# A fused transformer block and two hybrid layers on one core: norm roots on token columns, the key root one unit later, and another order in the second layer's lead

## The reference

```python
def rmsnorm(x, g):
    return x * lax.rsqrt(jnp.mean(x * x, axis=-1, keepdims=True) + 1e-6) * g
def first_block(...):
    h = rmsnorm(x, attn_pre_g)                       # stage "pre"
    ...                                              # attention of 16 heads
    x = x + rmsnorm(mix, attn_post_g)                # stage "post"
    h = rmsnorm(x, mlp_pre_g)                        # stage "mpre"
    y = (gelu(conv(h @ w_gate)) * (h @ w_up)) @ w_down
    x = x + rmsnorm(y, mlp_post_g)                   # stage "mpost"
    return x + (p @ w_ple) * sigmoid(x @ w_ple_gate)
def hybrid_layer(...):                               # two of them, on 16 meta tokens + 512
    h = rms_norm(x, norm_g)
    q, k, v, gate_a, u_b, gate_b, q_idx, k_idx, w_idx, merge = split(h @ w_in)
    q, k = rope(rms_norm(q)), rope(rms_norm(k)); q_idx, k_idx = rope(q_idx), rope(k_idx)
    score = sum_h relu(q_idx_h @ k_idx.T) * w_idx_h * scale
    sel = top_k(where(visible, score, -1e30), 128)
    attn = softmax over sel of (q @ k.T) @ v
    y_a = (attn * silu(gate_a)) @ w_a
    y_b = (multiscale_pool(u_b) * silu(gate_b)) @ w_b
    return x + (sigmoid(m_a) * y_a + sigmoid(m_b) * y_b) @ w_out
```

## Time and profile before

| | |
|---|---|
| median of 3 runs | 1642.54 us (1640.53 to 1642.84) |
| profiled execution, its own time | 1645.56 us |
| its span | 1643.6 us |
| granted TensorE clock, mean | 0.97 |
| PE busy | 1533.8 us (93%) |
| POOL busy | 1084.2 us (66%) |
| DVE busy | 945.4 us (58%) |
| ACT busy | 507.2 us (31%) |

### The profile page before, as it was taken

One profiled execution on the slowest core, in us unless ns is written; L12 is line 12 of the kernel. 1 busy time (PEld: TensorE's weight loads), 2 busy tenths in 40 slices (PEclk: granted clock), 3 DMA queues, 4 the chain that ended last, 5 costly groups with the idle time before them and its releaser, 6 DMA issues.

```text
span 1643.6 us, 26709 instructions
## 1 busy us (share of the span) xinstructions
PE 1533.8 (93%) x9622; PEld 1278.3 (78%) x9622; DVE 945.4 (58%) x2013; ACT 507.2 (31%) x1244; POOL 1084.2 (66%) x1700
## 2 busy tenths in 40 slices
PE   6989878979999999997999999999999988999999
PEld 4766544747777777885799988888999977788999
DVE  5544655067676763007686778863547769874251
ACT  3243565232111111003356333332125623333210
POOL 6542400749999998787987656445888853455685
PEclk9998988989999999998999999999999998999999
DMA  6120000212222223222222212111222211121223
GB/s 233 52 65 26 27 1 1 67 49 89 84 83 88 89 89 103 92 96 70 83 78 78 75 63 70 52 52 59 90 91 78 78 65 41 51 75 55 72 93 105
DMA packets 37351, 119.56 MB, mean 73 GB/s; under 512 B 5376, under 2 KB 7552, under 8 KB 36992
## 3 DMA queue, kind: packets, MB, share of 16 engines
q1 hardware_dynamic: 35824, 115.74, 21.2%
q10 hardware_dynamic: 1424, 2.41, 0.4%
HBM read 116.02 MB, written 2.10 MB: 72 GB/s over the span
## 4 chain that ended last, share of the span: by engine, by line
PE 70%; DVE 12%; POOL 8%; issue 4%; ACT 4%; DMA 0%; POOLq 0%; ACTq 0%; SPq 0%; DVEq 0%
PE ps L665 54%; POOL wlo L578 6%; PE ps L684 3%; POOL whi L574 2%; PE ps L1068 2%; DVE score L2100 2%; PE ps L824 2%; DVE score L2099 2%; PE ps L758 2%; PE ps L678 1%; PE ps L1143 1%; PE ps L691 1%; ACT pts L1337 1%; PE ps L1138 1%; ACT probs L1324 1%
## 5 line engine op out<-in xcount | busy, mean ns | idle before, releaser
L578 POOL TENSOR_TENSOR wlo<-raw,whi 128x256 fp32r<-128x256 f32 x752 | 606.4, 838 | 15.7
L574 POOL TENSOR_SCALAR whi<-raw 128x256 fp32r<-128x256 f32 x752 | 365.3, 512 | 364.4 <-PE ps L665 352.1
L665 PE MATMUL ps<-hh,whi 128*128 128x512 f32 (+2 forms) x1736 | 574.1, 331 | 25.8 <-DVE hl L1893 9.3
L665 PE MATMUL ps<-hl,whi 128*128 128x512 f32 (+2 forms) x1736 | 559.2, 322 | 0.0
L665 PE MATMUL ps<-hh,wlo 128*128 128x512 f32 (+2 forms) x1736 | 558.6, 322 | 0.0
L665 PEld LDWEIGHTS ps<-hh,whi 128*128 128x128 f32 x1736 | 329.3, 190 | 83.1 <-POOL wlo L578 27.4
L665 PEld LDWEIGHTS ps<-hh,wlo 128*128 128x128 f32 x1736 | 329.5, 190 | 25.8
L665 PEld LDWEIGHTS ps<-hl,whi 128*128 128x128 f32 x1736 | 329.4, 190 | 24.9 <-issue 2.2
L665 PE MATMUL ps<-plain_high,whi 128*128 128x264 f32 (+2 forms) x288 | 84.1, 292 | 6.3 <-POOL wlo L578 5.9
L1715 DVE TENSOR_TENSOR tmp<-tmp 128x512 f32<-128x512 f32 x14 | 9.7, 696 | 136.3 <-ACT tmp L1407 101.9
L684 PE MATMUL ps<-const,probs 128*128 128x128 f32 x360 | 67.7, 315 | 20.6 <-DVE probs L1874 20.0
(11 more groups left out here) (311 smaller groups left out, 2722.7 us busy)
## 6 DMA issues: line engine op xcount, KB each, us to landing
raw<-in_w SPq DMA_DIRECT2D x200, 512.0 KB, 3.3
x<-in_x SPq DMA_DIRECT2D x4, 512.0 KB, 6.9
out<-x SPq DMA_DIRECT2D x8, 256.0 KB, 6.3
raw<-in_w SPq DMA_DIRECT2D x12, 128.0 KB, 2.8
raw<-in_w SPq DMA_DIRECT2D x4, 384.0 KB, 3.1
cw_k<-in_cw1k SPq DMA_DIRECT2D x1, 1024.0 KB, 5.5
cw_v<-in_cw1v SPq DMA_DIRECT2D x1, 1024.0 KB, 8.3
raw<-in_w SPq DMA_DIRECT2D x4, 256.0 KB, 3.2
```

What stands on the lines that cost most here:

```text
L574: ins = pool.tensor_scalar(whi[s][:, c:c + PIECE], raw[s][:, c:c + PIECE], 1.0, 0.0, ALU.mult, ALU.add)
L578: ins = pool.tensor_tensor(wlo[s][:, c:c + PIECE], raw[s][:, c:c + PIECE], whi[s][:, c:c + PIECE].bitcast(F32), ALU.subtract)
L665: mm = pe.matmul(out, lhs, rhs, start=start and n == 0, stop=stop and n == 2)
```

## The change

1. The stages pre, post and mpost take their root on token columns. PE sums each token's squares with 128x1 matmuls (`token_sums`), ACT takes the root of 128x4, DVE the reciprocal of 128x4 into `small`, and PE spreads it back over the partitions into the PSUM tile X (`spread_root`, four matmuls of 128x128 with the identity). `norm` multiplies by X. In mpost the third unit of `embedded` stands between the sum and the spreading. Stage mpre stays as it was.
2. In both layers the ones matmul and ACT's 128x528 root go. The reciprocal is of 128x5, PE spreads it within the value unit (`spread_halves`, six matmuls of up to 128x128), and ACT copies it to `keep`. The squares of the key are summed in 5 columns before the first query unit, the key's root is taken on 128x5, and PE spreads it after the second query unit. `kiT` is written without it, and `kT` in two multiplications by X before chunk 2's rotation (`keys_out`).
3. In layer 1 the lead has an order of its own for PE, ACT and DVE; the selection of tile 2 leaves the lead and is dealt to slots 0 and 1; tile 3's side steps move from slots 0 to 4 to slots 2 to 5, and tile 4's from 5 to 9 to 6 to 9.

```diff
-                lead = rest + named("ga0 ga1") + two[0:1] + named("ga2") + score_first + two[1:2] + [("weighted", 0)]
-                lead += named("ga3") + two[2:3] + named("mg0") + two[3:] + named("mg1")
+                lead = ga[0:2] + two[0:1] + ga[2:3] + score_first + ga[3:] + two[1:2] + mg[0:1] + two[2:3] + mg[1:] + two[3:]
+                lead_act = ga[0:2] + two[0:1] + ga[2:] + score_first + two[1:2] + mg[0:1] + two[2:3] + mg[1:] + two[3:]
+                lead_dve = rest + ga[0:2] + score_first + two[0:1] + ga[2:3] + [("weighted", 0)] + ga[3:] + two[1:]
+                side[0] += picks[0:4]
+                side[1] += picks[4:]
-                spans = [(3, 0, 5), (4, 5, 10)]
+                spans = [(3, 2, 6), (4, 6, 10)]
...
+            def token_sums(tag, src, outs, start=True, stop=True):
+                for t, out in enumerate(outs):
+                    mm = pe.matmul(out, src[:, t * P:(t + 1) * P], ones[:, 0:1], start=start, stop=stop)
+                return mm
+            def spread_root(tag):
+                pe.wait_ge(*at("token_rstd", tag))
+                for t in range(QT):
+                    mm = pe.matmul(X[:, 0, t * P:(t + 1) * P], small[:, 13, t:t + 1].to_broadcast([P, P]), ident,
+                                   start=True, stop=True)
+                mm.then_inc(*tick("rstd_spread", tag))
...
-            def norm(tag, src, normed, cols, gain, r, out=None, then=None):
+            def norm(tag, src, normed, cols, gain, out=None, then=None):
+                r = X[:, 0, :]
                 dve.wait_ge(*at("rms", tag))
-                dve.reciprocal(r, r).then_inc(*tick("rstd", tag))
-                dve.wait_ge(*at("rstd", tag))
+                dve.reciprocal(small[:, 13, 0:QT], small[:, 12, 0:QT]).then_inc(*tick("token_rstd", tag))
+                dve.wait_ge(*at("rstd_spread", tag))
...
             embedded(1)
-            sum_added("mpost", [X[:, 0, :]], [tmp[:, 2, 0:S]])
-            for m in range(2, DC):
+            sum_added("mpost", tmp[:, 2, 0:S])
+            embedded(2)
+            spread_root("mpost")
+            for m in range(3, DC):
...
+                        if (m, k) == (L_V, 2):
+                            pe.wait_ge(*at("token_rstd", tag))
+                            spread_halves(r_tok).then_inc(*tick("rstd_spread", tag))
...
                     if c == 1:
+                        pe.wait_ge(*at("k_token", l))
+                        spread_halves(k_tok[2]).then_inc(*tick("k_spread", l))
...
+                def keys_out():
+                    dve.wait_ge(*at("k_spread", l))
+                    for half in (1, 0):
+                        ins = dve.tensor_tensor(halves(kT2[half * HD:(half + 1) * HD, :]), halves(kT2[0:HD, :]),
+                                                X[0:HD, :, 0:TH], ALU.mult)
+                    ins.then_inc(*tick("k_ready", (l, 1)))
```

125 lines of the change are left out of this document (76 added, 49 removed).

## The result

The change is slower: 1650.75 us median of 5 runs (1648.78 to 1651.20) against 1640.94 of 5 (1640.53 to 1642.84); ratio 1.0045, interval 1.0031 to 1.0060, so 5 to 10 us (the two medians lie 9.8 apart). The forecast was 1625. The profiled execution has a span of 1649.0 us against 1643.6, granted clock 0.97 in both. The change's profile lies at its median, that of the kernel before 3 to 5 us above its own, so the two profiles differ by 5.4 only.

What follows compares the result with a forecast made beforehand. PE, busy 93% of the span, was taken as the bound; terms -2.2 (pre), -3.3 (post), -1.6 (mpost), -2.0 (heads) and -8.5 (lead) gave -17.6, from 1642.54 to 1625 us median, range 1617 to 1634.

Steps and rivals of the forecast that it cites:

- Pre, -2.2: Stage pre: shorter root and reciprocal in PE's chain against an added spreading, -2.4, less 0.2 for the clock: -2.2 us.
- the columns cost what the ones matmul did: Stages pre, post, mpost: ten one-column passes cost PE 1.17 us against 1.16 for four wide ones.
- Post, -3.3: Stage post: shorter chain -2.4, two shorter norms -1.05, with +0.2 for the clock: -3.3 us.
- the +0.2 for the clock: Stage post: slower clock of PE behind idling, priced at +0.2 us.
- Mpost, -1.6: Stage mpost: DVE starts 2.4 us earlier, a wait of some 0.5 within `embedded`, only later waits shrink: -1.6 us.
- Heads, -2.0: Heads of both layers: PE work +3.6 us, waits shrink by 5.6: -2.0 us.
- three quarters of the 7.3 for gone: Heads of both layers: of 7.3 us that PE stands behind POOL and in a further wait, 5.6 go.
- Lead to slot 3, -8.5: Layer 1 lead: first stall -5.5, its clock -2.6, second stall -6.7, new slot 2 stall +4.8, relu waits +1.5: -8.5 us.
- Slots 4 to 10, 0: Layer 1 from slot 3 on: PE has no wait of note, as DVE's remaining slots carry less than PE's; no cost.
- The rival on the slower side: Layer 1: dealt selection delays tile 3's, PE stands at slot 6; needs DVE over 22 us behind; say 1646; chance 0.03.
- roots are hidden or dear: Stages and heads: spreadings cost more, heads +3.6, stages at half; about -8, 1634 us; chance 0.12.
- The signs that the forecast named for a wrong step: PE waiting over 1 us at `embedded` or the key's spreading; the new wait at slot 2 over 9 us or absent.

Runs made afterwards that it cites:

- the run without dealing: The change with tile 2's selection back in the lead in one piece and the old spans for tiles 3 and 4: 1642.09 us, ratio 0.9996 to the kernel before.
- the third part alone: The kernel before with only the change's layer 1 lead orders, dealing of tile 2's selection and spans: 1648.81 us, ratio 1.0031.
- the half rounds: The change with 8 of the 16 rounds of tile 3's selection in layer 1 left out: 1643.23 us, ratio 0.9998 to the kernel before.
- the slot more for tile 3: Kernel before with four of tile 2's rounds in the lead, rest in slot 0; tile 3 in slots 1 to 5 instead of 1 to 4: 1635.53 against 1640.53 us.
- the relus first: The change with ACT taking index (4)'s relus in slot 6 ahead of the eviction and exponentials: 1650.39 us, ratio 1.0041 to the kernel before.
- half a move: Kernel before with another lead: four of tile 2's rounds in the lead, four in slot 0, tile 3 in slots 1 to 5: 1635.53 us, ratio 0.9961.
- Pre only: The kernel before with only stage pre on token columns as in the change: 1644.69 us, ratio 1.0009.
- the runs with roots, pre or heads only: Change without its third part, 1645.59 us; kernel before with only the change's stage pre, 1644.69 us; kernel before with only its two layer heads, 1644.93 us.

## Why the prediction was wrong

- **Pre, -2.2, measured +2.7 to +3.0 in the seven profiles that have it, +1.4 (-1.0 to +3.8) in the median.** The failed step is "the columns cost what the ones matmul did", with 0.2 for an engine that had just idled. At equal pace it holds (1.7 us a chunk for either, 0.95 and 1.02 in mpost). But the row that it was taken from ran at full clock, and so did the last chunks of pre before, behind wide passes. With columns the pace never rose: eight passes at 0.213 us stand against two at 0.43. That is 0.85 us in each of five chunks, 4.2 in all, and the spreading took 2.07 where the sum had 1.03.
- **Post, -3.3, measured -1.5.** The mechanism was right: the reciprocal and the relief of the norms came (the first norm to PE's first product took 4.18 instead of 5.11 us). The term mis-sized is the +0.2 for the clock: the columns took 1.87 where the ones sum had 1.13, and the spreading 2.08 where the sum had 1.03, together 1.8. Where a later kernel met full clock here, post gave -2.3 to -4.3, so the size of this term is in part chance.
- **Mpost, -1.6, measured -2.5.** The wait within `embedded` was 0.17, not 0.5, and the norms took 0.73 to 0.75. The relief of DVE's norms, by row and rule, came as forecast.
- **Heads, -2.0, measured +0.9 in the sections, +2.6 (0.3 to 4.9) in the median.** The failed step is "three quarters of the 7.3 for gone". POOL's waits went as forecast (5.9 to 1.5 in both layers), but the wait for DVE's fourth rotated query stands at 1.7 in each layer, where only layer 1 had one, of 1.4. So 2.4 us of waiting went, not 5.6. PE's busy time grew by 0.9 and 2.3, 3.2 against the 3.6 that the sum had, although a spreading took 1.5 to the next start where 1.25 was taken. (Three quarters of 7.3 is 5.5, a slip of 0.1.)
- **Lead to slot 3, -8.5, measured -8.2.** First stall and its clock gone, the new stall in slot 2 at 5.4 against 4.8; by kinds, 6.5 of idle time and 1.7 of slower work, where the sum had 5.9 and 2.6.
- **Slots 4 to 10, 0, measured +13.7.** This decides. The failed step: "From slot 3 on PE has no wait of note, today nor then, since DVE's remaining slots carry less than PE's". The trace of the kernel before speaks against it: DVE was busy for 23.83 of the 24.90 us of slots 3 to 5. Tile 3 and tile 4 have four slots each instead of five, and index (4) moved into a slot where ACT and DVE are not free for it. Three waits of 2 us came of it, and half clock was priced at nothing: it cost more than the waits, 8.7 of busy time against 2.9 + 2.0 of idle time. About half of that slower work also came in the run without dealing, which has none of the new waits.
- The rival on the slower side named the right mechanism, later selections behind the dealt one, but expected a stall for tile 3's mask at slot 6 and put it beyond a backlog of 22 us. No such stall came: waits for `gate_out`, a relu and an eviction did it, with half clock. Its chance of 0.03 was too low. The rival "roots are hidden or dear" was right in pre and the heads. The signs that the forecast named for a wrong step (a wait of over 1 us at the spreadings or `embedded`, the new stall over 9 or absent) were not met, and none of them looked behind slot 2.

That dealing and spans make the change slower is shown by the times: the third part alone is +5.1, and without dealing the change is at -0.7. In the profiles the late sections then add 4.0 instead of 13.7, so the half clock there is not theirs alone. That the load on DVE is behind the rest is shown by the half rounds, which took some 7 us off the time; the slot more for tile 3 and the relus first agree with it. Open: whether pre costs what its trace shows, since putting it back did not speed up the median; where the half rounds' gain lies; and what sets the half clock in slots 6 to 11 of the run without dealing.

## What to carry to other kernels

Work that is moved out of a stall has to be followed to the end of every queue that it is put into, slot by slot: in a stretch where the receiving engine is 96% busy, as DVE was in slots 3 to 5, there is no room, whatever its share over the whole span. Allow for half clock as well: here 4.9 us of new waits came with 8.7 us of slower work, not all of it theirs. Deal a long piece over as many slots as keep the later pieces' slots as they were; half a move, which frees the waiting instruction in time and no more, with one slot more for the next piece, gave 6 us where the whole move lost 5. A reduction onto columns costs PE what the wide one does at the same clock, so it pays where it shortens the chain behind a sum and PE is at full clock; as PE's first work, in stage pre, it left PE at half pace where the wide passes did not. Take the level of the clock with every price that is carried from one place to another.

## What the runs showed of the hardware that was not expected

- A matmul with one moving column costs what a 128x128 one does. Its passes start 0.11 us apart at clock 1.00 (ten in 1.03 to the next instruction's start in the heads) and 0.21 at 0.50 (eight in 1.87 in post); eight passes of 128x128 took 1.03 and 2.08. Each pass has a new stationary tile of 128x128, and the weight loads were busy for 1.78 of the 1.87 us in post.
- One-column passes without a gap did not bring the clock up. In stage pre 64 of them ran from 7.46 us on at 0.213 each, the pace of half clock, and the 128x128 passes behind them took 2.07, again half clock. In the kernel before the 128x512 passes went from 0.85 to 0.43 apart at about 12.2 us, having begun at 7.50. The granted clock is given as 1.00 over all of this, for 8 to 11.8 us and for 13 to 17 us of the kernel before alike, though the pace differs by two. So in these first microseconds the lengths tell the level and the clock figure does not.
- The same wait is followed by half clock of different length. Before one group of index (3, 0)'s passes in layer 0 PE waited 1.11 us for relu in all of these. Window of 10 us from there, before:

```profile
968.00:978.00 10.00, 9.43 (x47) 7.22 (x48) 8.75 (x16) 4.07 (x9) 2.77 (x4) 0.83 0.16 53
```

The change:

```profile
966.00:976.00 10.00, 9.22 (x34) 6.63 (x35) 8.49 (x15) 3.97 (x10) 3.06 (x4) 0.66 0.15 53
```

Pre only:

```profile
971.00:981.00 10.00, 9.46 (x61) 7.42 (x61) 8.98 (x16) 4.20 (x11) 2.71 (x5) 1.00 0.18 55
```

The clock over them was 0.83, 0.66 and 1.00: 3.4 us of difference, for a wait of one length ahead of the same instructions. The attention, which no kernel changed, took between 4.8 us less and 0.2 more than before's 305.8 in the other profiles, about half of what separates the fastest and the slowest run of one kernel (before: 1639.3 to 1648.3, over three chips). Likewise the stretch from 1300 to 1383.1 us is the same in the kernel before and in the runs with roots, pre or heads only, and took 1.9 to 2.1 more in these, all of it busy time. So what the half clock behind a wait costs can't be priced from the wait, and a single profile does not settle a few us.
